# Even-layer mixer: state on two partition halves, output products of 128 rows, and a new order of projections and turns

## The reference, cut to what matters

```python
lam = lax.complex(s5_a_re, s5_a_im); dt = jnp.exp(s5_log_dt)[:, None]
lam_bar = jnp.exp(lam * dt)
b_bar = ((lam_bar - 1.0) / lam)[..., None] * b_mat
bu = jnp.einsum('gnc,btgc->btgn', b_bar, uf)
h = linear_scan(jnp.broadcast_to(lam_bar, bu.shape), bu, h0)
y = jnp.einsum('gcn,btgn->btgc', c_mat, h).real + s5_d * uf
```

## Time and profile before

| | us |
|---|---|
| median of 3 runs | 583.68 |
| lowest, highest | 582.53, 586.0 |
| the profiled execution's own time | 583.62 |
| its span, first to last instruction | 581.2 |
| TensorE busy in the span | 556.1 |
| VectorE, ScalarE, GpSimd busy | 247.2, 156.2, 86.6 |

### The profile page before, as it was taken

How to read it: one execution, slowest core, us unless ns; L and a number is a source line. 1 busy time by engine, 2 the same in 40 slices (tenths; PEclk the granted TensorE clock), 3 DMA queues, 4 the chain that set the end, 5 groups by cost and what they waited for, 6 DMA issues and landing times. The chain is left out here.

```text
span 581.2 us, 8487 instructions
## 1 busy us (share of the span) xinstructions
PE 556.1 (96%) x3422; PEld 307.2 (53%) x3422; DVE 247.2 (43%) x559; ACT 156.2 (27%) x331; POOL 86.6 (15%) x116
## 2 busy tenths in 40 slices
PE   6999999999999999999999999999999889999994
PEld 4777876543633333337876555667654533333331
DVE  6999783223751112154633415260113642221146
ACT  7131295121301101143235104154004220101114
POOL 5991800000112110000000001000000012120000
PEclk9999999999999999999999999999999999999998
DMA  8996999897999999999999998999699999999972
GB/s 330 419 359 86 244 392 386 359 409 296 370 411 419 421 421 418 384 291 396 386 416 325 419 377 324 317 353 413 257 390 421 380 407 417 420 419 420 374 244 92
DMA packets 40809, 208.94 MB, mean 360 GB/s; under 512 B 12931, under 2 KB 14659, under 8 KB 25440
## 3 DMA queue, kind: packets, MB, share of 16 engines
q1 hardware_dynamic: 31296, 169.93, 75.1%
q0 software_dynamic: 7872, 34.53, 16.3%
q10 hardware_dynamic: 1600, 3.90, 1.7%
HBM read 198.77 MB, written 43.74 MB: 417 GB/s over the span
## 5 line engine op out<-in xcount | busy, mean ns | idle before, releaser
L1521 PE MATMUL bank<-arena 128*64 128x512 f32 x264 | 85.7, 598 | 0.5 <-DVE arena L1872 0.5
L1521 PE MATMUL bank<-ring,arena 128*64 128x512 f32 x232 | 74.7, 598 | 0.1
L2337 PE MATMUL bank<-arena,ring 128*128 128x320 f32 x256 | 71.6, 434 | 0.0
L2337 PEld LDWEIGHTS bank<-arena,ring 128*128 128x128 f32 x256 | 48.0, 190 | 21.4 <-issue 1.6
L1442 PE MATMUL bank<-ring,arena 128*128 128x512 f32 x92 | 40.3, 594 | 1.0 <-PEq L455 0.6
L1521 PEld LDWEIGHTS bank<-arena 128*64 128x64 f32 x264 | 24.0, 136 | 31.5 <-issue 31.4
L1552 PE MATMUL bank<-arena 128*64 128x512 f32 x136 | 39.8, 594 | 0.7 <-ACT arena L1761 0.7
L577 PE MATMUL bank<-xnT,ring 128*128 128x320 f32 x144 | 39.5, 434 | 0.7 <-DVE xnT L897 0.7
L1988 DVE COPY arena<-bank 128x512 f32<-128x512 f32 x14 | 9.7, 691 | 68.3 <-PE bank L1552 68.3
L1552 PE MATMUL bank<-ring,arena 128*64 128x512 f32 x120 | 36.1, 593 | 0.7 <-ACT arena L1761 0.7
L1521 PEld LDWEIGHTS bank<-ring,arena 128*64 128x64 f32 x232 | 20.8, 136 | 24.5 <-issue 24.3
(11 more groups left out here) (455 smaller groups left out, 851.4 us busy)
## 6 DMA issues: line engine op xcount, KB each, us to landing
arena<-in_w_moe SPq DMA_DIRECT2D x50, 1024.0 KB, 16.4
ring<-in_w_moe SPq DMA_DIRECT2D x44, 1024.0 KB, 15.1
arena<-in_stream_b SPq DMA_DIRECT2D x4, 2560.0 KB, 15.2
out_o_d_old<-in_cache_d_g POOLq DMA_DIRECT2D x1, 8448.0 KB, 29.8
arena<-in_stream_a SPq DMA_DIRECT2D x4, 2048.0 KB, 10.4
out_o_d_old<-in_cache_d_g POOLq DMA_DIRECT2D x1, 7680.0 KB, 38.9
out_o_d_old<-in_cache_d_g SPq DMA_DIRECT2D x1, 4608.0 KB, 38.0
ring<-in_w_out_even SPq DMA_DIRECT2D x2, 2048.0 KB, 7.8
```

The lines of the kernel that those rows point to most:

```text
L1521: last = nc.tensor.matmul(c.bank[2 + j % 2][half, :], xgT[:, j % 2, q, half], w[i][q // 4][:, q % 4, :], start=(q == 0), stop=(q == KC - 1))
L2337: last = nc.tensor.matmul(bank(name)[:, 0:TOK], w[:, k, i * P:(i + 1) * P], xnT[:, k, :], start=(k == 0), stop=(k == KC - 1))
```

## The change

The state is laid out anew for the output products: partitions 0 to 63 hold the real part, 64 to 127 the imaginary part, and the group of the pair (`par`) takes the place of `r` in the free dimension. `H`, `cp` and `bbd` follow. The output product over the state is then one matmul over 128 rows for each group. For it `cp` is made from two forms of the output matrix, one as before but in the new layout (`c_own`) and one with the halves exchanged (`c_other`, prepared on the host as `s5_c_swapped` and loaded by a transfer of its own), and from `pwn`, powers with signs, that ScalarE copies from `pw`. ScalarE takes over the copies into `bbd`. TensorE's q3 goes ahead of the chunk states, half of the second outputs ahead of the turns of p0, and the turns of p1 and z0 to z3 and the banks of the last jobs are put in another order. On ScalarE o0 goes ahead of y2 and y3; on VectorE the copy of pS goes between the two halves of the second normalisation.

```diff
@@ -280,13 +280,13 @@
...
 BANK_JOBS = ["x0a", "x0b", "x1a", "x1b", "x2a", "x2b", "u0", "u1", "u2", "u3", "q0", "w0", "w1", "w2", "w3", "w4", "w5", "w6", "w7",
-             "q1", "q2", "tau", "V00", "V10", "V01", "V11", "q3", "k", "v", "s0A", "s0B", "sSA", "sSB", "s1a", "s1b",
-             "s1c", "s1d", "y0", "y1", "p0A", "p0B", "y2", "y3", "pS", "pN", "o0", "p1a", "p1b", "p1c", "p1d",
-             "z0", "z1", "z2", "z3", "oS0", "oS1", "o1", "oT", "g0", "g1", "g2", "g3"]
+             "q1", "q2", "tau", "q3", "V00", "V10", "V01", "V11", "k", "v", "s0A", "s0B", "sSA", "sSB", "s1a", "s1b",
+             "s1c", "s1d", "y0", "y1", "p0A", "p0B", "y2", "y3", "pS", "pN", "o0", "p1a", "p1b", "z0", "p1c", "p1d",
+             "z1", "z2", "z3", "oS0", "oS1", "o1", "oT", "g0", "g1", "g2", "g3"]
 ACT_JOBS = ["u0", "u1", "u2", "u3", "q0", "w0", "w1", "w2", "w3", "w4", "w5", "w6", "w7", "q1", "q2", "tau", "q3", "k", "v",
-            "y0", "y1", "p0A", "p0B", "y2", "y3", "o0", "p1a", "p1b", "p1c", "p1d", "o1", "g0", "g1", "g2", "g3"]
-LATE_BANKS = {"p1c": 3, "p1d": 2, "z0": 5, "z1": 4, "z2": 6, "z3": 7, "oS0": 3, "oS1": 2, "o1": 5, "oT": 4,
-              "g0": 6, "g1": 7, "g2": 3, "g3": 2}
+            "y0", "y1", "p0A", "p0B", "o0", "y2", "y3", "p1a", "p1b", "p1c", "p1d", "o1", "g0", "g1", "g2", "g3"]
+LATE_BANKS = {"p1a": 6, "p1b": 7, "z0": 3, "p1c": 5, "p1d": 4, "z1": 2, "z2": 3, "z3": 6, "oS0": 7, "oS1": 5, "o1": 4, "oT": 2,
+              "g0": 3, "g1": 6, "g2": 7, "g3": 5}
 BANK_OF = [LATE_BANKS[name] if name in LATE_BANKS else n % 8 for n, name in enumerate(BANK_JOBS)]
...
             "s1c", "s1d", "pS", "pN", "z0", "z1", "z2", "z3", "oS0", "oS1", "oT"]
@@ -333,6 +333,8 @@
...
     two = Carve(c.ring, 3 * SLOT, 2 * SLOT + 4 * 512)
+    t["c_other"] = c.ring[:, 3 * SLOT - 512:3 * SLOT].rearrange("p (a j c) -> p a j c", a=2, c=GC)
+    t["pwn"] = c.arena[:, 1280:1280 + 4 * PAIRS * (CH + 1)].rearrange("p (f a j k) -> p f a j k", f=2, a=2, j=PAIRS)
     t["U"], t["H"], t["t1"] = two.take(G, NCH), two.take(2, PAIRS, NCH), two.take(2, PAIRS, PCH)
...
     hb = 2 * SLOT + 4 * 512 + G * NCH
@@ -421,8 +423,9 @@
...
     logdt, a_re, a_im = (ev["in"][:, PAIRS * q:PAIRS * (q + 1)] for q in range(3))
-    braw, ct = (ev["in"][:, 3 * PAIRS + 512 * q:3 * PAIRS + 512 * (q + 1)].rearrange("p (r j c) -> p r j c", r=2, c=GC)
+    braw, c_own = (ev["in"][:, 3 * PAIRS + 512 * q:3 * PAIRS + 512 * (q + 1)].rearrange("p (r j c) -> p r j c", r=2, c=GC)
                 for q in range(2))
+    c_other, pwn = ev["c_other"], ev["pwn"]
     late = ev["late"]
...
     sinks, sinks_s = late[:, 2 * SK:2 * SK + A_H], late[:, 2 * SK + A_H:2 * SK + A_H + 2]
@@ -463,6 +466,7 @@
...
             c.load_item(sp, IT_QKV)
+            sp.dma_start(c_other, x["s5_c_swapped"].rearrange("p (a j c) -> p a j c", a=2, c=GC)).then_inc(ld_bc, 16)
             sp.dma_start(late, x["even_late"]).then_inc(ld_late, 16)
...
             sp.dma_start(vc, x["vc_a"]).then_inc(ld_kc, 16)
@@ -545,7 +549,7 @@
...
             grow(ph, 1, 0)
-            g.memset(ev["f1"], 0.0).then_inc(ph_ok, 1)
+            g.memset(sm[24], 0.0).then_inc(ph_ok, 1)
             g.memset(wuu, 0.0).then_inc(wuu0, 1)
...
             pool.wait_ge(ld_late, 16)
@@ -611,11 +615,12 @@
...
             for i in range(4):
-                for r in range(2):
+                for par in range(2):
                     for q in range(4):
-                        last = nc.tensor.matmul(bank("tau")[32 * q:32 * q + 32, i * P:(i + 1) * P], bbd[:, r, 4 * i + q, :],
-                                                cp[:, r, 4 * i + q, 0:P], start=(r == 0), stop=(r == 1))
+                        last = nc.tensor.matmul(bank("tau")[32 * q:32 * q + 32, i * P:(i + 1) * P], bbd[:, par, 4 * i + q, :],
+                                                cp[:, par, 4 * i + q, 0:P], start=(par == 0), stop=(par == 1))
             last.then_inc(full, 1)
+            project("q3", lambda k: wq[:, k, 3 * P:4 * P])
...
             emptied(pe, "w7")
@@ -628,7 +633,6 @@
...
                     last.then_inc(full, 1)
-            project("q3", lambda k: wq[:, k, 3 * P:4 * P])
             project("k", lambda k: wq[:, k, 4 * P:5 * P])
...
             claim(pe, "v")
@@ -668,29 +672,53 @@
...
                 last.then_inc(full, 2)
-            def outputs(ih):
+            def outputs(ih, first, end):
                 tiles = (2 * ih, 2 * ih + 1)
-                claim(pe, f"y{tiles[0]}")
-                claim(pe, f"y{tiles[1]}")
-                for q in range(4):
+                if first == 0:
+                    claim(pe, f"y{tiles[0]}")
+                    claim(pe, f"y{tiles[1]}")
+                for q in range(first, end):
                     for i in tiles:
...
                     pe.wait_ge(h_ok, 2)
-                    for r in range(2):
-                        for i in tiles:
-                            for par in range(2):
-                                rows = slice(64 * par, 64 * par + 64)
-                                last = nc.tensor.matmul(bank(f"y{i}")[64 * par:64 * par + NCH, q * P:(q + 1) * P],
-                                                        H[rows, r, 4 * i + q, :], cp[rows, r, 4 * i + q, GC:],
-                                                        start=False, stop=(r == 1))
-                last.then_inc(full, 2)
+                    for i in tiles:
+                        for par in range(2):
+                            last = nc.tensor.matmul(bank(f"y{i}")[64 * par:64 * par + NCH, q * P:(q + 1) * P],
+                                                    H[:, par, 4 * i + q, :], cp[:, par, 4 * i + q, GC:],
+                                                    start=False, stop=True)
+                if end == 4:
+                    last.then_inc(full, 2)
+            def probs_turned(n):
+                claim(pe, "p1" + "abcd"[n])
...
+            def out_ahead(h, first, end):
...
+            def y_turned(i):
+                claim(pe, f"z{i}")
+                for s in range(CH):
+                    last = nc.tensor.transpose(bank(f"z{i}")[:, s * NCH:(s + 1) * NCH], y40[:, i, s], c.ident[0:NCH, 0:NCH])
+                last.then_inc(full, 1)
             pe.wait_ge(wuu_in, 16 * 16)
-            outputs(0)
+            outputs(0, 0, 4)
+            outputs(1, 0, 2)
             claim(pe, "p0A")
...
             pe.wait_ge(p_ok["0"], 1)
@@ -698,7 +726,7 @@
...
                     last.then_inc(full, 1)
-            outputs(1)
+            outputs(1, 2, 4)
             claim(pe, "pS")
...
             pe.wait_ge(p_ok["S"], 1)
@@ -713,31 +741,21 @@
...
             last.then_inc(full, 1)
-            for n in range(4):
-                if n % 2 == 0:
-                    pe.wait_ge(p_ok["1"], 1 + n // 2)
-                claim(pe, "p1" + "abcd"[n])
...
+            pe.wait_ge(p_ok["1"], 1)
+            probs_turned(0)
+            probs_turned(1)
+            emptied(pe, "y1")
+            y_turned(0)
+            emptied(pe, "o0")
+            c.arrived(pe, IT_OUT_E)
+            out_ahead(0, 0, 2)
+            pe.wait_ge(p_ok["1"], 2)
+            probs_turned(2)
+            probs_turned(3)
+            y_turned(1)
             emptied(pe, "y3")
-            for i in range(4):
-                claim(pe, f"z{i}")
-                if i == 2:
-                    emptied(pe, "o0")
-                    c.arrived(pe, IT_OUT_E)
-                    out_ahead(0, 0, 2)
-                for s in range(CH):
-                    last = nc.tensor.transpose(bank(f"z{i}")[:, s * NCH:(s + 1) * NCH], y40[:, i, s], c.ident[0:NCH, 0:NCH])
-                last.then_inc(full, 1)
+            y_turned(2)
+            y_turned(3)
             emptied(pe, "pN")
...
             for half in range(2):
@@ -815,6 +833,21 @@
                 act.dma_start(x["u_rows"][i * P:(i + 1) * P], uT[:, i, :]).then_inc(u_out, 16)
+                if i == 0:
+                    act.wait_ge(pw_ok, 1)
+                    for par in range(2):
+                        mine = slice(64 * par, 64 * par + 64)
+                        nc.scalar.copy(pwn[0:64, 0, par], pw[mine, 0])
+                        nc.scalar.activation(pwn[0:64, 1, par], pw[mine, 1], ACT.Copy, scale=-1.0)
+                        nc.scalar.activation(pwn[64:P, :, par], pw[mine], ACT.Copy, scale=-1.0)
+                if i == 2:
+                    act.wait_ge(bbd0, 1)
+                    act.wait_ge(wt_ok, 1)
+                    for par in range(2):
+                        for r in range(2):
+                            last = nc.scalar.copy(bbd[64 * r:64 * r + 64, par, :, par * GC:(par + 1) * GC],
+                                                  bbar[64 * par:64 * par + 64, r])
+                    last.then_inc(bbd_ok, 1)
             def queries(i):
...
                 filled(act, f"q{i}")
@@ -863,11 +896,11 @@
...
             exps("1", A_H, lambda h: S1[:, h, :])
-            y_rows(2)
-            y_rows(3)
             filled(act, "o0")
...
```

(52 more changed lines are left out.)

19 lines of the change are left out of this document (9 added, 10 removed).

## The result

The changed kernel took **590.03 us** (median of 5 runs, 588.86 to 592.72), the kernel before 583.68 (5 runs beside them, 582.53 to 586.50): ratio **1.0116 [1.0085, 1.0146]**, slower by 6.35 us. The forecast was 587.0 with a range up to 589.8. Its sign was right, its mechanism in the mixer too; more than half of the excess came from a place that the prediction had called unchanged. The profiled execution took 592.72, span 590.8.

A forecast was written before the change was run, and what follows sets the result against it. TensorE, busy 96% of the span, was taken as the bound, so any shift of the mixer's end shifts the span's end. Terms +7.8 - 0.9 - 0.6 + 0.1 - 3.2 = +3.2 gave 587.0 us; 8-in-10 range 583.2 to 589.8.

The forecast's parts named there:

- Part 1: Mixer's start: `c_other` lands behind w_qkv at 22.4, so VectorE's table products start then, not at 14.64: +7.8 us.
- Part 2: Mixer's tables: `bbd` copies go from VectorE to ScalarE, -0.9 us; `wt` ready at 38.8, `cp` at 54.1.
- Part 3: TensorE until the scores: waits 4.2 us for `wt`, 3 for `cp`, none for U; scores 6.4 us late.
- Part 4: Mixer's output products and softmax: 16 equal records per q and the new order gain 3.2 us, bounds 2 to 4.
- Sum: Whole kernel: +7.8 - 0.9 - 0.6 + 0.1 - 3.2 = +3.2 us, giving 587.0 us.
- (A): Mixer's start: `c_other` slips past w_qkv and lands by 14.6, so the change gains: 579.5 us, chance 0.10.
- (B): Mixer: TensorE's clock falls in its new holes of 4.2 and 3.0 us: 589.3 us, chance 0.17.
- (C): Behind the mixer: delayed cache copies press transfers together and hold up the experts' weights: 590.5 us, chance 0.05.

The follow-up runs named there:

- after: The changed kernel itself, with the whole change, against the kernel before: 590.03 us, ratio 1.0116.
- e1_wait_moved: Changed kernel with VectorE's wait for `c_other` moved from the first table product to ahead of the `cp` products that read it: 584.73 us, ratio 1.0022.
- f3_moved_twice: Changed kernel with VectorE's wait for `c_other` moved later and each product of U and its table issued twice (128 instructions more): 581.52 us, ratio 0.9963.
- e2_fill32: Changed kernel with 32 tiny unread matmuls (128 instructions) in TensorE's idle time at the start: 588.91 us, ratio 1.0082.
- e3_both: Changed kernel with both edits, VectorE's wait for `c_other` moved later and 32 tiny matmuls at the start: 581.25 us, ratio 0.9950.
- f1_before_fill32: Kernel before, without the change, with 32 tiny matmuls (128 instructions) ahead of TensorE's first transposes: 587.42 us, ratio 1.0079.
- f2_moved_fill64: Changed kernel with VectorE's wait for `c_other` moved later and 64 tiny matmuls (256 instructions) at the start: 588.02 us, ratio 1.0078.
- g1_twice_fill32: Changed kernel with the `c_other` wait moved later, products of U issued twice and 32 tiny matmuls at the start (256 instructions more): 586.69 us, ratio 1.0055.
- g2_moved_fill16: Changed kernel with VectorE's wait for `c_other` moved later and 16 tiny matmuls (64 instructions) at the start: 584.81 us, ratio 1.0014.
- h1_q3_back: e3_both with the third query projection, q3, put back behind the state products as in the kernel before: 580.25 us, ratio 0.9942.
- f4_warm_fill: Changed kernel with 25 tiny matmuls at the start and 7 products of 256 columns in TensorE's wait ahead of the table turns: 589.31 us, ratio 1.0103.

## Why the prediction was wrong, point by point

**Part 1** held: landing 22.4 forecast, first product at 22.08 after; the term is +7.4, not +7.8. e1_wait_moved takes it back alone (first product at 15.26).

**Part 2** held: `wt` 38.27 (38.8), `cp` 53.46 (54.1). ScalarE's copy of u3 came at 35.51 (36), and U was there in time: no hole stands before the state products, which start at 59.94.

**Part 3** gave the right sum for half a wrong reason. The hole before the turns was 3.65 (4.2), before tau 1.23 and not 3: the clock fell in the first and stretched the turns by 1.7 us, which the second took up. The four writes of the state took 3.81 us together against 1.8 for two. Their mean, 0.95, is above the 0.88 that I had as the bound, but it comes from the last one: they took 0.87, 0.83, 0.83 and 1.23. VectorE and not TensorE was what set the scores, at +6.38 (6.4).

**Part 4** held: gain 2.87 (3.2, bounds 2 to 4), 0.87 us for a q (0.88). The sentence that it "does not depend on whether the products save 3.5 or 5.5" fits f3_moved_twice, where 3.5 us given back cost 0.46.

**Sum.** The mixer: +3.5 against +3.2 (583.7 + 3.2 is 586.9; the 587.0 is rounded up). **The step that failed** is the one before all the parts: "by whatever time the mixer ends sooner or later, the span ends sooner or later", with no term for what lies behind. Removing 128 TensorE instructions made the branch at the end of the expert stage 2.3 us longer. e2_fill32 and e3_both put 128 other instructions in and the hole goes; f1_before_fill32 adds 128 to the kernel before, without the change, and a hole of 3.37 comes. In the wait list of the kernel before this hole was 0.9 us long and I had read it as nothing; it was ended by a sequencer and not by data, and such a row says nothing on how long it will be in another program. 3.5 + 2.3 = 5.8 of the 6.35 measured.

**The remainder** is put down to the clock, from profiles and records, not by an experiment of its own: in the six kernels with a long hole the median lies 0.5 to 2.9 us above the sum, 1.4 on the mean (0.55, 1.3, 1.7, 1.0, 2.9, 1.1); in the seven with a short one -0.7 to +1.5, mean 0.1. That behind a long hole the clock falls in some executions is seen in after, f2_moved_fill64, g1_twice_fill32 and g2_moved_fill16, and it did not in the profiles of e1_wait_moved and f1_before_fill32. From run to run of most kernels the time goes with the clock: the twelve of e1_wait_moved span 582.27 us at 0.997 to 586.98 at 0.985. But not every fall belongs to the hole. Four profiles have one in an expert stage, with no hole over 1.1 us near it: after at 168.6, f1_before_fill32 at 466.6, f3_moved_twice at 461.7, h1_q3_back at 463.6. In f3_moved_twice and h1_q3_back the hole at the branch was a short one.

**The rivals.** (A) did not happen by itself; its mechanism is e1_wait_moved and e3_both. Its own arithmetic, 579.5, stands against 581.25 with the hole mended: without the wait the stage came 2.8 us sooner than before (e1_wait_moved), not 4.1, for the scores came no sooner. (B) was right that the clock falls in the mixer's first hole and that this costs little there, and f4_warm_fill shows its second half: at tau it costs 1.3 us, where 2 to 3 were forecast. What I had not seen is that the costly falls would be at the stage's end. The rule cited for it (the Trainium skill, TensorE: Matmul & The Clock Gate, "HAM oscillation — how this bites in real kernels"), that a waiting TensorE starts its next burst at half rate, agrees with the turns of 5.38 us and with tau's 3.22; it does not tell these from the products behind the holes of 3.13 and 3.37 us in e1_wait_moved and f1_before_fill32, which ran at full rate (10.64 us). (C) fell: the stage that waits for weights took 160.3 to 161.0 us from start to last product in every kernel without a fall in it, whether it began at 110 or at 119.
